# Query-tile changes get a projection tile between their index products; the head steps of the sparse attention get fewer blocks

## The reference

```python
def attend(args):                       # one block of queries
    ql, qi, wi, qc = args
    s = jnp.einsum("bqhd,bkd->bqhk", qi, k_idx)                  # index products, 8 heads, depth 64
    score = jnp.einsum("bqhk,bqh->bqk", jax.nn.relu(s), wi).astype(f32)
    allowed = cid[None, :] <= qc[:, None]                        # chunks of 64 tokens, causal
    score = jnp.where(allowed[None], score, -jnp.inf)
    top_s, top_i = lax.top_k(score, top_k)                       # the best 128 keys of each query
    ...
    logits = jnp.einsum("bqhc,bqkc->bqhk", ql, kv).astype(f32)   # 8 heads, latent depth 128
    logits = jnp.where(valid[:, :, None, :], logits, -jnp.inf)
    prob = jax.nn.softmax(logits, axis=-1).astype(kv.dtype)
    return jnp.einsum("bqhk,bqkc->bqhc", prob, kv)
```

## Time and profile before

| what | value |
|---|---|
| median of 3 runs | 3597.56 us (3595.7 to 3604.61) |
| the profiled execution | 3588.09 us, span 3586.4 us |
| mean granted TensorE clock | 0.975 of full speed |
| PE, PEld busy | 96%, 86% of the span |
| DVE, ACT, POOL busy | 43%, 33%, 34% |

### The profile page before, as it was taken

The page is one execution under the profiler, slowest core; times in us unless marked ns, Lnnn a source line. Parts: engine busy times, 40 slices in busy tenths (PEclk is TensorE's granted clock), DMA queues, the critical chain, the costliest instruction groups (busy, mean ns, idle before and its releaser), DMA issues. The chain is left out here.

```text
span 3586.4 us, 74703 instructions
## 1 busy us (share of the span) xinstructions
PE 3428.6 (96%) x30266; PEld 3101.0 (86%) x30266; DVE 1527.1 (43%) x2694; ACT 1187.2 (33%) x2257; POOL 1221.6 (34%) x912
## 2 busy tenths in 40 slices
PE   8999999998989999999999999999989899999998
PEld 8999999777768999999999999987767677878886
DVE  5331234445776344332053313344557763453312
ACT  3222352112554334222232223521235533342222
POOL 4444335210002343544434443342100114534442
PEclk9999999998999999999999999999989999999999
DMA  3332222001111332332223332220021113323332
GB/s 96 91 91 87 73 65 59 3 3 51 45 30 36 80 92 66 94 91 87 81 80 91 91 90 63 73 50 3 3 54 42 38 28 91 95 73 94 94 93 72
DMA packets 464412, 236.59 MB, mean 66 GB/s; under 512 B 20862, under 2 KB 462476, under 8 KB 464156
## 3 DMA queue, kind: packets, MB, share of 16 engines
q1 hardware_dynamic: 464156, 232.92, 23.1%
HBM read 230.50 MB, written 2.10 MB: 65 GB/s over the span
## 5 line engine op out<-in xcount | busy, mean ns | idle before, releaser
L558 POOL TENSOR_TENSOR W_low<-W,W_high 128x512 fp32r<-128x512 f32 (+1 forms) x544 | 720.4, 1325 | 879.5 <-ACT W_high L631 878.8
L153 PE MATMUL PS<-u_high,W_high 128*128 128x264 f32 (+1 forms) x3040 | 934.5, 307 | 11.4 <-DVE u_low L421 8.0
L154 PE MATMUL PS<-u_low,W_high 128*128 128x264 f32 (+1 forms) x3040 | 925.2, 304 | 0.0
L155 PE MATMUL PS<-u_high,W_low 128*128 128x264 f32 (+1 forms) x3040 | 924.7, 304 | 0.0
L631 ACT ACTIVATE W_high<-W 128x512 fp32r<-128x512 f32 (+1 forms) x544 | 335.6, 619 | 990.8 <-PE PS L155 953.4
L153 PEld LDWEIGHTS PS<-u_high,W_high 128*128 128x128 f32 x3040 | 575.1, 189 | 42.7 <-DVE u_low L421 10.4
L154 PEld LDWEIGHTS PS<-u_low,W_high 128*128 128x128 f32 x3040 | 575.3, 189 | 25.4
L155 PEld LDWEIGHTS PS<-u_high,W_low 128*128 128x128 f32 x3040 | 573.1, 189 | 24.1
L153 PE MATMUL PS<-u_high,dW_high 128*128 128x264 f32 (+1 forms) x1280 | 387.8, 303 | 9.9 <-ACT pj_ml L1656 3.9
L154 PE MATMUL PS<-hidden_low,W_high 128*128 128x264 f32 (+1 forms) x1232 | 369.9, 300 | 0.0
L155 PE MATMUL PS<-hidden_high,W_low 128*128 128x264 f32 (+1 forms) x1232 | 368.9, 299 | 0.0
(11 more groups left out here) (362 smaller groups left out, 5481.4 us busy)
## 6 DMA issues: line engine op xcount, KB each, us to landing
W<-in_ffn_w_in SPq DMA_DIRECT2D x352, 256.0 KB, 3.0
W<-in_ffn_w_out SPq DMA_DIRECT2D x160, 256.0 KB, 2.8
dW<-in_w_in SPq DMA_DIRECT2D x156, 256.0 KB, 2.9
W<-in_w_in SPq DMA_DIRECT2D x96, 256.0 KB, 3.0
W<-in_w_branch SPq DMA_DIRECT2D x48, 256.0 KB, 3.0
W<-in_w_out SPq DMA_DIRECT2D x32, 256.0 KB, 3.0
W<-in_ffn_w_out SPq DMA_DIRECT2D x32, 128.0 KB, 2.2
xt<-in_x SPq DMA_DIRECT2D x4, 512.0 KB, 4.5
```

Source lines behind the costliest of these rows:

```text
L153: nc.tensor.matmul(dst, wh, xh, start=first, stop=False)
L154: nc.tensor.matmul(dst, wh, xl, start=False, stop=False)
L155: return nc.tensor.matmul(dst, wl, xh, start=False, stop=final)
L558: g.tensor_tensor(WL[:, r, 0:nk], W[:, r, 0:nk], WH[:, r, 0:nk].bitcast(F32), ALU.subtract).then_inc(S("split"), 1)
```

## The change

Eight blocks (one output tile) are put into the turn of stages 1, 2 and 3: four behind the index products of heads 2 and 3, four behind those of heads 4 and 5. The head steps get 24 blocks in stages 0 to 2 in place of 28, and 16 in stage 3, two per step. The total stays 128. ACT evacuates that tile and rounds two more weight units behind the relus, and DVE splits one unit before it starts the scoring.

```diff
--- before.py
+++ after.py
@@ -1661,11 +1661,13 @@
 
 
             START = (8, 4, 4)
-            TWO, THREE = ((2, 2), (2, 2)), ((1, 2), (1, 2), (1, 1))
-            PER_STEP = (TWO + THREE + TWO + TWO + THREE + TWO + TWO) * 2 + ((0, 0),) * H
+            TURN = (0, 8, 8, 8, 0)
+            TWO, THREE, FOUR = ((2, 2), (2, 2)), ((1, 2), (1, 2), (1, 1)), ((1, 1),) * 4
+            PER_STEP = (THREE + THREE + TWO) * 3 + FOUR * 2 + ((0, 0),) * H
             share = lambda e: PER_STEP[e]
-            given_after = [sum(START) + sum(sum(share(i)) for i in range(e + 1)) for e in range(NQ * H)]
-            assert given_after[-1] == 16 * KD
+            given_after = [sum(START) + sum(TURN[0:e // H + 1]) + sum(sum(share(i)) for i in range(e + 1))
+                           for e in range(NQ * H)]
+            assert given_after[-1] == dense.tiles * KD
 
             def spans(nk):
                 return ((0, min(nk, 512)),) + (((512, nk),) if nk > 512 else ())
@@ -1778,10 +1780,12 @@
                         if j + 1 < NQ:
                             index(j, 2)
                             index(j, 3)
-                            if j == 0:
-                                dense.blocks(pe, START[2])
-                            for hd in range(4, H):
-                                index(j, hd)
+                            dense.blocks(pe, TURN[j] // 2 if j else START[2])
+                            index(j, 4)
+                            index(j, 5)
+                            dense.blocks(pe, TURN[j] // 2)
+                            index(j, 6)
+                            index(j, 7)
                             logits(j, 0)
                             logits(j, 1)
                         for hd in range(H):
@@ -1867,6 +1871,8 @@
                                 dense.after(act, sum(START))
                             for hd in range(4, H):
                                 relus(j, hd)
+                            if j:
+                                dense.after(act, given_after[j * H - 1] + TURN[j])
                         else:
                             values_out(j - 1, H // 2 - 1)
                         exponentials(j, 0)
@@ -1928,6 +1934,8 @@
                         nk = t0 + n
                         more = j + 1 < NQ
                         if more:
+                            if j:
+                                dense.lows(v, dense.RING + given_after[j * H - 1] // dense.UK)
                             scores(j + 1)
                         def maxima(hd):
                             e = j * H + hd
@@ -1960,7 +1968,7 @@
                                 maxima(hd + 2)
                             if more:
                                 select(j + 1)
-                            dense.lows(v, dense.RING + (given_after[e - 1] if e else sum(START)) // dense.UK)
+                            dense.lows(v, dense.RING + (given_after[e - 1] + (TURN[j] if hd == 0 else 0) if e else sum(START)) // dense.UK)
                         if more:
                             nk1 = sum(QT[j + 1])
                             b1 = bias[:, (j + 1) % 2]
```

## The result

The changed kernel takes 3628.58 us (median of 9 runs, 3608.55 to 3636.43) against 3594.7 us (9 runs, 3582.36 to 3604.93): a ratio of 1.0093, 95% interval 1.0077 to 1.011, slower by 34 us. The prediction said 3607 and a range up to 3619.

The account below looks back on a forecast made before the run. DVE's chain was taken to pace stages 2 and 3 wholly, stage 1 nearly, PE stage 0. Turns at +14.75 and +16.05 us, less 10.1 given back per layer, made about +10: 3607 us, range 3595 to 3619.

Parts of the forecast that it names:

- The turns get longer: Turns of stages 1 to 3: scoring waits behind the moved blocks on PE, +14.75 us in layer 1, +16.05 in layer 2.
- DVE sets the end: Attention phase: DVE's chain sets the pace of stages 2 and 3 wholly, of stage 1 nearly; PE leads in stage 0.
- Rival A: Whole phase: PE sets the end, so only its half-clock and idle time count; faster, 3582 us, chance 0.09.
- The sum in which half of the throttled time of the turns comes back: Three half-clock stretches of 6.8 us give back 10.2 us, not the 1.3 credited; the total is then about +2.
- The head steps give back 10.1 us per layer: Head steps with fewer blocks get shorter: stage 0 by 3.1 us, stage 1 by 1.7, stage 2 by 1.4, stage 3 by 3.9.
- both terms: Stage 3's head steps: five splits become three, -1.2 us, and the end behind the last reciprocal shortens, -2.7; together -3.9.
- the tail: From DVE's last reciprocal in stage 3 to ACT's first exponential of stage 4: 6.5 us before, 3.8 forecast, so -2.7.
- the prediction's list of stretches: Three stretches at 1.2 GHz, 6.8 us each: at 905.30, at 2690.50 and in layer 1's stage 2 turn.
- Rival B: Stage 3's head steps: with twelve blocks less the clock drops there, costing 19 us over both layers; 3626 us, chance 0.06.
- the row of stage 4: Evidence against a clock drop: stage 4 is busy 17.96 us of 24.20 without any block and keeps PEclk 0.98.
- Time outside the phase: Sign against the prediction: the whole is wrong if time changes outside the attention phase.
- The evacuation and roundings behind the relus cost nothing: ACT's extra work before its first exponential, about 0.6+0.5+0.5 us, fits in 2.5 us of idle time.

Follow-up runs that it names:

- experiment 2: Kernel before, with 24 filler matmuls behind the index products of heads 3 and 5 in the turns of stages 1 to 3, no block moved: 3624.43 us, ratio 1.0087.
- experiment 6: Kernel before, with six filler matmuls behind the index products of heads 3 and 5 in the turns of stages 1 to 3: 3592.55 us, ratio 1.002.
- experiment 3: Changed kernel, its 24 turn blocks put ahead of the first index product, head-step table kept, splits distributed differently: 3629.31 us, ratio 1.0099.
- experiment 10: Changed kernel with at most one weight split per head step on DVE: 3609.81 us, ratio 1.005.
- experiment 5: Changed kernel with filler matmuls in the head steps of stages 1 to 3, only as many as fit PE's waits for probabilities: 3604.3 us, ratio 1.0035.
- experiment 9: Changed kernel with filler only in the first head step of stage 2 and the first two of stage 3: 3610.71 us, ratio 1.0049.
- experiment 4: The change in stages 0 and 1 alone, stages 2 and 3 as in the kernel before with 28 blocks each: 3601.45 us, ratio 1.0025.
- experiment 11: Kernel before with the splits of weight units 20 to 31 on POOL, the others on DVE: 3589.03 us, ratio 0.9992.
- experiment 8: Changed kernel with this phase's weight splits on POOL in place of DVE: 3606.13 us, ratio 1.003.
- experiment 1: Changed kernel with eight filler matmuls in each head step of stages 2 and 3, ahead of PE's wait for probabilities: 3620.97 us, ratio 1.0093.
- experiment 7: Kernel before with this phase's weight splits on POOL in place of DVE: 3589.99 us, ratio 1.0003.

## Why the prediction was wrong

*The turns get longer: right.* Forecast +14.75 and +16.05 us, measured +15.7 and +17.0. Experiment 2 shows the same price without any block leaving the head steps.

*DVE sets the end: right, as long as the clock holds.* Rival A (faster, 3582) is excluded by the result itself and by experiment 2, where PE's arithmetic allows +20 us and the phase took +29.2. The sum in which half of the throttled time of the turns comes back (+2) is out as well: stage 2's turn differs by 1.3 us between the layers, for 5.1 us at half clock (experiment 6). Half clock doubles PE's own work (logits of 0.83 us took 1.70); how much of that reaches the kernel's end depends on who waits for it. In the dense stretch of experiment 3, 20.5 us at half clock cost 10.3.

*The head steps give back 10.1 us per layer: wrong, and this is the step that failed.* They gave back 0.15 and 0.1: stage 0 1.9 of 3.1, stage 1 0.7 of 1.7, stage 2 lost 0.7 where 1.4 were due, stage 3 lost 1.7 and 1.9 where 3.9 were due. These 20 us are most of the 24 that the forecast lacked to the measured +34, and 11.4 of them are stage 3's.

For stage 3 both terms were right as long as the clock held: with one split per step (experiment 10) the reciprocals came 1.24 us sooner (-1.2 for two splits) and the tail shrank by 2.84 (forecast 2.7), together 38.04 us for the 38.2 of the sum. What the sum put at nothing is the clock: the prediction priced a split at 0.6 us wherever it stands, and did not see that its table puts two into the first head step. They push DVE's second reciprocal back, PE then waits 2.7 us for probabilities, the clock falls, and half-clock logits make DVE wait 4.1 us in sum. So the reciprocals took 3.3 us longer than before instead of 1.2 less, and the tail gave 1.6 instead of 2.7. Experiment 5 takes the clock out and leaves the pair: 39.0 us. Experiment 10 takes the pair out: 38.0. For stage 2 the same two runs give 37.45 and 37.2 us where the sum has 36.8, so 0.4 to 0.6 of its 1.4 stay missing.

For stage 0, 6.8 us at half clock (from 873.0 us; 3.4 before, from 871.2, which the prediction's list of stretches leaves out) stand beside the missing 1.2 us. Where PE leads, as it does there, half of the 3.4 more would be 1.7; that is an estimate, and no run isolates it. For the missing 1.0 of stage 1 I have no account.

*Rival B named the mechanism but mis-stated its trigger.* It gave the clock loss in stage 3 a chance of 0.06, on the row of stage 4, where PE is as little busy and keeps its clock. That row says nothing of waits: those of stage 4's head steps are at most 1.0 us each. And B laid it to the two blocks per step, which experiment 3 clears: there the same table runs stage 3 at 1.00. Its time of 3626 us is near the measured 3628.58 partly by luck: it asked for 19 us in stage 3, where 11.4 were lost, and stages 0 to 2 lost most of the rest. The range ended where B should have been taken in.

*Time outside the phase.* The prediction called itself wrong as a whole if time changed there. In the profiled execution 8 us did, in unchanged code and in a stretch that some executions have and others not (below); the phase's own +32.4 shows that the miss does not hang on it.

*The rest.* The evacuation and roundings behind the relus cost nothing: the first exponential of stage 3 starts 1.13 us behind the memset in both kernels (1011.04-1009.91, and 995.09 less 993.96 in the earlier trace rows). The turns of stages 1 and 3 are 0.5 us longer here than in experiment 2, that of stage 2 is not; the evacuation at the end of the last head step may be the reason, which no run shows. No engine waited for a DMA in the phase.

What stays open: why the clock falls in some places of like activity and not in others. In stage 3 it held behind waits of 2.25, 1.51, 2.12 and 1.52 us in experiment 3, fell behind a single one of 2.11 in experiment 9, and in experiment 10 fell behind the first, of 2.24, but not behind one of 2.10. So the pair of splits is shown as what costs the time, and the long waits as what has to be filled or shortened, but not a rule for when the clock goes. Open too are the shares of stages 0 and 1.

## What to carry to other kernels

Work moved onto a chain that another engine waits for costs its full length, and comes back elsewhere only where the engine that gives it up was leading. Before counting on the thinner place, look at the single waits that PE gets there and at what waits for PE behind them, not only at its mean busy share: the granted clock may go (here it went to 0.84 over a stage with waits of 2.24 and 2.71 us in successive steps), and then the waits grow on both sides. Price that as part of the range, since the runs here give no sure sign of it. Where a helper batches catch-up work ("up to this count"), see in which step the change makes two fall together.

## What the runs showed that I had not expected

Useless matmuls in PE's waits made the changed kernel's median 24 us shorter, 13 of them in the phase (experiment 5). The run time of one kernel follows the granted clock: of the nine runs of the changed kernel the fastest had a mean of 0.974 and took 3608.55 us, the slowest 0.964 and 3636.43. Single stretches of 20.5 us at 1.2 GHz turn up in unchanged code in some profiled executions (between 2217 and 2235 us in the changed kernel and experiments 2, 4 and 11, near 434 us in experiments 3, 8 and 9) and not in others (the kernel before, experiments 1, 5, 6, 7 and 10). So sections of a trace say more than its total. Against the kernel before, us, both layers' phases and all the rest of the profiled execution:

| kernel | phases | the rest |
|---|---|---|
| changed | +32.4 | +8.0 |
| 1, filler everywhere | +31.9 | -6.5 |
| 2, turns alone | +29.2 | +10.3 |
| 5, filler in waits | +19.4 | -3.2 |
| 8, changed, POOL | +13.8 | +11.4 |
| 9, filler first | +25.3 | +3.3 |
| 10, one split per step | +17.4 | +1.5 |
| 11, hybrid | -4.5 | +11.6 |

PEclk was 1.00 in every turn that got runs of matmuls, of 24 as of 6, where those of stage 1 and of layer 1's stage 2 had been at 0.83 to 0.87 and 0.67.
